# Two feed-forwards with seven-product tiles: products accumulated in one bank, a norm factor carried by the next epsilon

## The reference, cut to what matters

```python
hn = rmsnorm(h, pre_ffn_norm)
ff = (jax.nn.silu(hn @ w_gate) * (hn @ w_up)) @ w_down
h = h + rmsnorm(ff, post_ffn_norm)
e = rmsnorm(p @ w_ple_proj, ple_norm)
gate = jax.nn.sigmoid(h @ w_ple_gate + b_ple_gate)
h = h + e * gate
```

## Time and profile before

| | us |
|---|---|
| median of 3 runs | 1558.11 |
| the runs | 1557.65 to 1559.58 |
| span of the profiled execution | 1558.7 |
| PE busy in it | 1535.3 |
| DVE busy | 1064.5 |
| ACT busy | 715.5 |
| first feed-forward, seven-product tiles | 554.5 to 705.7 |
| second feed-forward, first matmul of its units | about 1144 |

### The profile page before, as it was taken

One profiled execution on the slowest core, in us unless ns is written; L12 is line 12 of the kernel. 1 busy time (PEld: TensorE's weight loads), 2 busy tenths in 40 slices (PEclk: granted clock), 3 DMA queues, 4 the chain that ended last, 5 costly groups with the idle time before them and its releaser, 6 DMA issues.

```text
span 1558.7 us, 19501 instructions
## 1 busy us (share of the span) xinstructions
PE 1535.3 (98%) x7464; PEld 1270.6 (82%) x7464; DVE 1064.5 (68%) x1657; ACT 715.5 (46%) x1069; POOL 133.7 (9%) x131
## 2 busy tenths in 40 slices
PE   8999899999999999999999999999999999999998
PEld 3788677877888899998888787878888888888877
DVE  8998898898888799995753456766476444432356
ACT  5543578764543656653333325446354322222233
POOL 0111000000000111110021011100201101000000
PEclk9999999999999999999999999999999999999999
DMA  9778222233666546657333323111332222323331
GB/s 367 183 187 206 69 94 61 75 95 93 210 238 203 163 127 158 157 148 253 98 110 101 108 85 109 55 41 41 115 132 99 95 95 95 108 86 101 98 135 68
DMA packets 59709, 197.18 MB, mean 127 GB/s; under 512 B 7005, under 2 KB 9309, under 8 KB 59234
## 3 DMA queue, kind: packets, MB, share of 16 engines
q1 hardware_dynamic: 52208, 175.49, 34.3%
q0 software_dynamic: 7408, 20.46, 6.6%
q10 hardware_dynamic: 2, 0.00, 0.0%
HBM read 171.80 MB, written 6.30 MB: 114 GB/s over the span
## 4 chain that ended last, share of the span: by engine, by line
PE 89%; DVE 7%; ACT 2%; issue 1%; DMA 1%; ACTq 0%; POOL 0%; DVEq 0%; POOLq 0%
PE bank L1822 22%; PE bank L1814 22%; PE bank L1815 22%; PE bank L1852 3%; PE bank L1844 3%; PE bank L1843 3%; DVE convout L2430 2%; PE bank L1870 2%; DVE tmp L2501 1%; PE bank L1882 1%; PE bank L1884 1%; PE bank L1883 1%; PE bank L1957 1%; PE bank L1974 1%; DVE spl L2376 1%
## 5 line engine op out<-in xcount | busy, mean ns | idle before, releaser
L1814 PE MATMUL bank<-HH,sph 128*128 128x512 f32 x1192 | 475.7, 399 | 6.9 <-DVE spl L2376 4.7
L1815 PE MATMUL bank<-HH,spl 128*128 128x512 f32 x1192 | 466.0, 391 | 0.0
L2376 DVE TENSOR_TENSOR spl<-raw,sph 128x1024 fp32r<-128x1024 f32 (+1 forms) x206 | 259.8, 1263 | 225.0 <-ACT sph L2032 224.9
L2032 ACT ACTIVATE sph<-raw 128x1024 fp32r<-128x1024 f32 (+1 forms) x227 | 233.0, 1029 | 176.6 <-PE bank L1822 139.5
L1822 PE MATMUL bank<-HL,sph 128*128 128x512 f32 x1192 | 309.7, 394 | 0.0
L1814 PEld LDWEIGHTS bank<-HH,sph 128*128 128x128 f32 x1192 | 225.0, 189 | 58.9 <-issue 10.2
L1815 PEld LDWEIGHTS bank<-HH,spl 128*128 128x128 f32 x1192 | 224.9, 189 | 47.8 <-issue 1.5
L1822 PEld LDWEIGHTS bank<-HL,sph 128*128 128x128 f32 x1192 | 222.7, 188 | 48.6 <-issue 2.4
L2430 DVE SCALAR_TENSOR_TENSOR convout<-convin,vecs,convout 128x512 f32<-128x512 f32 x240 | 165.3, 748 | 0.0
L1814 PE MATMUL bank<-midh,sph 128*128 128x512 f32 x352 | 136.9, 389 | 0.0
L1815 PE MATMUL bank<-midh,spl 128*128 128x512 f32 x352 | 136.9, 389 | 0.0
(11 more groups left out here) (362 smaller groups left out, 2281.0 us busy)
## 6 DMA issues: line engine op xcount, KB each, us to landing
raw<-in_w_in SPq DMA_DIRECT2D x69, 512.0 KB, 3.6
raw<-in_w_up SPq DMA_DIRECT2D x66, 512.0 KB, 3.5
more<-in_w_ada SPq DMA_DIRECT2D x32, 512.0 KB, 5.0
raw<-in_w_down SPq DMA_DIRECT2D x32, 512.0 KB, 3.5
raw<-in_w_gate SPq DMA_DIRECT2D x22, 512.0 KB, 3.2
spl<-raw POOLq DMA_DIRECT2D x18, 512.0 KB, 6.0
ada<-in_w_ada SPq DMA_DIRECT2D x16, 512.0 KB, 10.9
raw<-in_w_down SPq DMA_DIRECT2D x16, 384.0 KB, 3.1
```

The costliest lines, as they stand in the source:

```text
L1814: e.matmul(P_[b][:], sph(n)[:, q], hi[:, k, :], start=k == 0, stop=False)
L1815: e.matmul(P_[b][:], spl(n)[:, q], hi[:, k, :], start=False, stop=False)
L2032: e.activation(sph(n), raw(n), ACT.Copy).then_inc(*up("s_w_high", ("wh", n)))
L2376: e.tensor_tensor(spl(n), raw(n), sph(n).bitcast(F32), ALU.subtract).then_inc(*up("s_w_low", ("wl", n)))
```

## The change

- The second feed-forward gets seven-product tiles too, tiles 4 to 17 (`SEVEN`).
- The seven products of a tile come in the order 0, 3, 2, 4, 5, 1, 6 (`SEVEN_STEP`). Products 0, 2, 5 and 6 are accumulated in one half bank, 3 and 4 in another, 1 beside it. Between them the running sum is copied out (`seven_first`, `seven_third_copy`, `seven_second` on ACT) or added (`seven_up` on DVE), and the next product of that sum waits for it. Two pairs of banks take turns. `factors` makes the factors in the new order; the gate unit's raw buffer is given back later.
- In the second feed-forward `seven_full` makes the scaled x for the T sums, eight instructions on ACT, four behind the root and four behind unit 4; `halves_2(n)` hands out the T sums behind units 3 to 6 and `seven_third` behind 5 and 7. The T operands lie on x, so x is written to DRAM before (`x_spill_all`, SP) and read back after (`x_reload(2)`, POOL).
- Up is no longer multiplied by r (`up_`). The down product is then ff / r, and the same result comes from the epsilon EPS / r^2 in its norm, which `eps_row` stores; `rsqrt` takes it for the name `ff`. In the seven-product tiles `seven_row` multiplies the gate by r.
- The embedding's squares go from the up stage to the down stage, read from a copy that is loaded again from DRAM (`e_copy`, SP).

```diff
-SEVEN = {1: (3, 18)}
+SEVEN = {1: (3, 18), 2: (4, 18)}
+SEVEN_STEP = (0, 3, 2, 4, 5, 1, 6)
 SEVEN_SUMS = (2, 3, 4)
-SEVEN_BANK = ((0, 0), (1, 0), (1, 1), (2, 1), (3, 1), (2, 0), (3, 0))
...
     def factor_low(st, s):
         add("seven_low", st["which"], s)
-        if s % 7 == 6:
+        if s % 7 >= 5:
             load()
+
+    def factor_high(st, s):
+        add("seven_high", st["which"], s)
+
+    def factor_sum(st, s):
+        add("seven_sum", st["which"], s)
 
     def factors(st, count):
         while st["made"] < min(count, st["total"]):
             s = st["made"]
-            if s % 7 in SEVEN_SUMS:
-                add("seven_sum", st["which"], s)
-                if s % 7 == 4:
-                    load()
-            add("seven_high", st["which"], s)
-            if s % 7 == 4:
+            pos = s % 7
+            if pos == 2:
+                factor_sum(st, s)
+                factor_sum(st, s - 1)
+                factor_high(st, s - 1)
+            elif pos == 3:
+                factor_sum(st, s)
+            if pos != 1:
+                factor_high(st, s)
+            if pos in (3, 4):
                 factor_low(st, s - 2)
-            if s and s % 7 != 3:
+            if s and pos not in (2, 3):
                 factor_low(st, s - 1)
...
-    def rsqrt(name, src, n, scale, after):
-        v, q, r = scratch(n), scratch(n), scratch(n)
-        add("rsqrt", name, src, v, q, r, n, scale, after)
+    def rsqrt(name, src, n, scale, after, eps=None):
+        v = scratch(3 * n)
+        q, r = v + n, v + 2 * n
+        add("rsqrt", name, src, v, q, r, n, scale, after, eps)
...
+        r = rsqrt(ss.name, ss.sums(b), T, 1.0 / width, [("cols", ss.name)], eps_row if ss.name == "ff" else None)
...
+        def sum_bank(i):
+            return banks[i % 2]
+
+        def pair_bank(i):
+            return banks[2 + i % 2]
+
+        def settle(pos, i):
+            if pos == 0:
+                add("seven_gate", which, i, pair_bank(i)[0], gate[i])
+            elif pos == 1:
+                add("seven_row", which, i, gate[i])
+            elif pos == 2:
+                add("seven_silu", which, i, gate[i])
+            elif pos == 3:
+                add("seven_mid", which, i, f0 + i, sum_bank(i)[0], gate[i], up[i])
+                tmp.give(up[i], ("seven_mid", which, i))
+            elif pos == 4:
+                add("seven_mid_high", which, i, f0 + i, gate[i])
+            elif pos == 5:
+                add("seven_mid_low", which, i, f0 + i, gate[i])
+                tmp.give(gate[i], ("hi", f"m{which}", f0 + i), ("lo", f"m{which}", f0 + i))
...
         for s in range(total):
-            i, step = divmod(s, 7)
+            i, pos = divmod(s, 7)
+            if pos == 1:
+                gate[i], free = tmp.take()
+                add("seven_first", which, i, sum_bank(i)[0], gate[i], free)
+            elif pos == 2:
+                up[i], free = tmp.take()
+                add("seven_third_copy", which, i, pair_bank(i)[0], up[i], free)
+            elif pos == 3:
+                add("seven_second", which, i, sum_bank(i)[0], gate[i])
+            elif pos == 5:
+                add("seven_up", which, i, sum_bank(i)[0], up[i])
+            if i:
+                settle(pos, i - 1)
             factors(st, s + 6)
             W["cut"] = max(W["cut"], st["first"] + (st["made"] + 1) // 2)
...
-            if step == 5 and i + 2 < f1 - f0:
+            if pos == 5 and i + 2 < f1 - f0:
                 add("seven_third", which, i + 2)
...
+            add("seven", which, s, sum_bank(i), pair_bank(i))
...
-        if which == 2:
-            jobs = [(*job[:3], e_squares) if 4 <= n < 13 else job for n, job in enumerate(jobs)]
-        if not st:
-            gemms(jobs, acts, 1 + which, hook=hook)
-            return
         f0, f1 = SEVEN[which]
...
+        def halves_2(n):
+            if n in (2 * f0 - 3, 2 * f0 - 1):
+                add("seven_third", which, (n - 2 * f0 + 3) // 2)
+            if n == 3:
+                add("seven_t_sum", which, 0)
+                add("seven_t_sum", which, 1)
+                add("seven_t_high", which, 0)
+            elif n == 4:
+                add("seven_t_low", which, 0)
+                add("seven_t_sum", which, 3)
+                add("seven_t_high", which, 1)
+            elif n == 5:
+                add("seven_t_low", which, 1)
+                add("seven_t_sum", which, 2)
+                add("seven_t_high", which, 3)
+            elif n == 6:
+                add("seven_t_low", which, 3)
+                add("seven_t_high", which, 2)
+                add("seven_t_low", which, 2)
...
+        if which == 1:
+            gemms([(*job[:3], lambda n=n: halves(n)) for n, job in enumerate(jobs[:2 * f0])], acts, 2,
+                  table="silu_table")
+        else:
+            gemms([(*job[:3], lambda n=n: halves_2(n)) for n, job in enumerate(jobs[:2 * f0])], acts, 3, hook=hook)
...
     def ffn_rows():
         ss = SumSq("x4")
         for i in range(8):
             ss.add(("XT", i), [("x", 4, i)])
+        add("x_spill_all")
         yield 2
         r = root_of(ss, D)
+        add("eps_row", eps_row, r - 8)
+        for i in range(4):
+            add("seven_full", 2, i)
 
...
         rate[0] = 0
+        for i in range(4, 8):
+            add("seven_full", 2, i)
...
         for i in range(8):
-            sse.add(("EE", i), [("e", i)])
+            sse.add(("EC", i), [("e_copy",)])
...
-    e_sums = e_sum()
-
-    def e_squares():
-        next(e_sums, None)
...
+    add("x_reload", 2)
     ssf = SumSq("ff")
     for i in range(8):
+        if i == 1:
+            add("e_copy")
+            side.append(e_sum())
+            rate[0] = 1
         if i == 7:
+            flush()
+            rate[0] = 0
             add("root_table", keepc(1))
         gemm("w_down", i, NFT, "m2", branch("FFO", i, ssf))
...
+            def x_spill_all():
+                w.wait_ge(at("x_back", 1), *[at("x", 4, i) for i in range(8)])
+                e.dma_start(A["x_scratch"], XT[:]).then_inc(
+                    *up("d_xs2", *[("x_spilt", 2, i) for i in range(8)], by=16))
+
+            def e_copy():
+                w.wait_ge(at("e_spilt"), at("e0_spilt"), *fenced("d2"))
+                e.dma_start(EC[:], A["e_scratch"]).then_inc(*up("d_ec", ("e_copy",), by=16))
...
+            def seven(which, s, sums, pairs):
+                i, step = s // 7, step_of(s)
+                whole_sum, pair = P_[sums[0]][:, 0:256], P_[pairs[0]]
+                to = {1: pair[:, 0:256], 3: pair[:, 256:512], 4: pair[:, 256:512]}.get(step, whole_sum)
+                begins = step in (0, 1, 3)
+                if step == 0:
+                    w.wait_ge(*(each(sums[1]) if i < 2 else [at("seven_mid", which, i - 2)]))
+                elif step == 3:
+                    w.wait_ge(*(each(pairs[1]) if i < 2 else [at("seven_gate", which, i - 2)]))
+                elif step == 2:
+                    w.wait_ge(at("seven_first", which, i))
+                elif step == 4:
+                    w.wait_ge(at("seven_third_copy", which, i))
+                elif step == 5:
+                    w.wait_ge(at("seven_second", which, i))
+                elif step == 6:
+                    w.wait_ge(at("seven_up", which, i))
...
             def seven_full(which, i):
+                if which == 2:
+                    w.wait_ge(at("x", 4, i), *fenced("f2"))
+                    e.activation(PF[:, i, :], XT[:, i, :], ACT.Copy, scale=vec("g_pf", i)).then_inc(
+                        *up("s_cut_a", ("full", 2, i)))
+                    return
...
+                if which == 2:
+                    w.wait_ge(at("e_spilt"))
...
+
+            def eps_row(a, v):
+                w.wait_ge(at("rs1", "x4"))
+                e.tensor_scalar(keep(a, T), sm(v, T), EPS, None, ALU.mult).then_inc(*up("s_scale", ("eps_row",)))
 
...
             def seven_t_sum(which, t):
-                w.wait_ge(*[at("full", i) for i in range(8)], *[at("lo", "n2", i) for i in range(8)], at("e0_spilt"),
-                          *[at("x_spilt", i) for i in range(8)])
+                w.wait_ge(*[at("full", which, i) for i in range(8)], *[at("x_spilt", which, i) for i in range(8)])
+                if which == 1:
+                    w.wait_ge(*[at("lo", "n2", i) for i in range(8)], at("e0_spilt"))
+                else:
...
+                if step == 2:
                     w.wait_ge(at("raw", n + 1), at("seven_third", which, s // 7))
                     ins = e.tensor_tensor(to, raw_half(n + 1, 0), raw_half(n + 1, 1), ALU.add)
-                elif s % 7 == 3:
+                elif step == 3:
+                    w.wait_ge(at("raw", n), at("seven_sum", which, s + 1))
+                    ins = e.tensor_tensor(to, sum_of(which, s + 1), raw_half(n, 0), ALU.subtract)
+                else:
                     w.wait_ge(at("raw", n), at("seven_sum", which, s - 1))
```

(32 more changed lines are left out.)

198 lines of the change are left out of this document (77 added, 121 removed).

## The result

The changed kernel takes 1566.95 us (median of 4 runs, 1566.47 to 1567.23) against 1558.62 for the kernel before: ratio 1.0051, 95% interval 1.0037 to 1.0064. The prediction was 1555.5 with 1561.5 as its upper end. The change costs 8.3 us where a gain of 2.6 was forecast. The profiled execution took 1566.47, with a span of 1564.7 us.

The account below looks back on a forecast made before the run. TensorE, busy 1535.3 of 1558.7 us, was taken as the bound. 1558.7 - 11.2 + 0.6 + 7.2 + 0.8 = 1556.1 us for the profiled execution, 1555.5 for the median; range 1548.0 to 1561.5.

Parts of the forecast that it names:

- Term 1: Products of the second feed-forward's 14 tiles: 10.08 instead of 10.88 us a tile, 11.2 us less.
- The rule of the smaller gap: The skill page's isolated matmul gap, N/2.4 + 2.5 ns, applied to the 14 tiles: 16.6 us saved in all.
- R2: Rival: all step-in cost is hidden, or tiles take 9.6 us; 1546.9 to 1549 us, chance 0.12.
- Term 2: Steady seven-product tiles: the new order's waits for running-sum copies all fit; no cost, 10.08 us a tile kept.
- R3: Rival: in steady tiles a later adding DMA holds PE each tile; 1564.2 us at 0.3 a tile, chance 0.08.
- Term 3: Stepping into the first feed-forward's tiles: third product waits for the copy of product one; 0.6 us.
- Term 4: Stepping into the second feed-forward's tiles: PE waits at unit 7, second and third product, plus adding DMAs; 7.2 us.
- R1: Rival: the second feed-forward's step-in costs half or less, 4 us; 1551.5 us, chance 0.32.
- drain: Skill page's 1.38 us at every ScalarE table switch; not expected here, if real the step-in sum 1.4 us higher.
- Moved and hidden: Spill and reload of x, weight loads, root, embedding's squares and transposes: zero each; 2 us if the copy's cover were gone.
- R4: Rival: the spill of x lands at 1183.9, 6 us after the first T sum wants it; 1561.5 us, chance 0.06.
- Term 5: Low clock behind the second feed-forward's step-in waits: 0.8 us taken, bounds 0 and 2.1.

Follow-up runs that it names:

- e9: e7 with POOL holding the low parts of the second and third undivided unit until VectorE's T sum is done; 1553.01 us.
- e3: Changed kernel with the second feed-forward's first four full products queued ahead of the norm row's root instead of behind it; 1563.10 us.
- e1: Changed kernel with the second feed-forward given back its old schedule, so the new one is in the first only; 1564.94 us.
- e2: Changed kernel with the older tile's banks handed out first where a stage's seven-product tiles end; 1560.87 us.
- e8: e1 with the edit of e2 added (new schedule in the first feed-forward only, exit's banks reordered); 1560.57 us.
- e4: Changed kernel with the embedding's sums (transposes into columns and root) four pieces later in the second feed-forward's down stage; 1564.86 us.
- e11: e7 with the last undivided tile's multiply and rounding queued behind the first seven-product tile's second product; 1556.07 us.
- e7: Changed kernel with the edits of e2, e3, e4 and e6, and both step-in adding transfers one weight unit earlier; 1553.31 us.
- e5: The changed kernel itself, unaltered, measured again; 1566.01 us.
- e6: Changed kernel with the third and fourth T low parts of the second feed-forward moved behind the first tile's weight sums; 1561.78 us.

## Why the prediction was wrong

**Term 1, products: right.** 11.1 to 11.4 by the balance above, 10.9 by e9 (U7 to Y 149.05 instead of 158.25, with 1.72 of waits in it), against 11.2. The rule of the smaller gap that I weighed beside it (16.6 in all) is refuted for this kernel, and R2 with it. (R2 had a slip besides: the 1550.1 that this rule gives lies outside R2's own 1546.9 to 1549.)

**Term 2, steady state: right.** R3, the adding transfer, is refuted: PE is gapless in both stretches. Only the very first tile waited for it (0.88; I had given 0.3 with a bound of 1.9). DVE's row of the sum that held `seven_up` there:

```profile
1209.96 0.69 DVE L2746 TENSOR_TENSOR sums<-raw 128x512 f32<-128x512 f32 x1 [2.88 <-DMA raw<-raw]
```

**Term 3, first step-in: right.** 0.64 against 0.6.

**Term 4, second step-in: right in kind, and right in sum by luck.** Unit 7: 1.61 against 2.0. Second product: 3.65 against 2.8 + 0.3. Third: 0.40 against 1.8. Adding transfer 0.88 against 0.3. Together 6.54 against 7.2. Up to the first T sum the forecast held to 0.2 us, once the 4.74 us by which U3 now comes later are taken off: the full products began at 1171.83 - 4.74 = 1167.09, the first Silu at 1179.09 - 4.74 = 1174.35 (forecast 1174.5), the first T sum at 1182.77 - 4.74 = 1178.03 (1177.9). Two steps behind it failed. I took both engines' durations as they are alone: three T operations at 1.23, of which two took 2.21 and 2.32 (1184.03 and 1192.32 in the changed kernel), some 2 us of DVE queue. The trace of before shows it, and I had not read those rows. DVE's rows there with POOL at work and with POOL idle, and POOL's:

```profile
1183.08 1.37 DVE L2382 TENSOR_TENSOR tmp<-tmp,tmp 128x512 f32<-128x512 f32 x1 [1.22 <-ACT tmp L2047]
...
1187.41 0.69 DVE L2382 TENSOR_TENSOR tmp<-tmp,tmp 128x512 f32<-128x512 f32 x1 [1.22 <-ACT tmp L2047]
...
1182.61 1.30 POOL L3061 TENSOR_TENSOR midl<-tmp,midh 128x512 fp32r<-128x512 f32 x1 [4.02 <-ACT midh L2243]
```

The Trainium skill (GPSIMD Engine Reference, Key points) says that GpSimd shares its SBUF interfaces with VectorE, with contention for instructions that have two SBUF inputs. The rows agree: both T sums and this square-sum have two such inputs.

And I followed the queues of DVE and ACT but not the banks: unit 5 needs the bank of unit 0's gate, whose reader the full products hold up (e3). That gave 1.40, in no term. R1 asked for a step-in of at most half and falls. The table load brought no drain here either: it starts at 1177.80, where the full product ahead of it ends (1175.23 + 2.55).

**"Moved and hidden", the step that cost most.** Zero for each, and the list did not have the exits at all. The exit of the first feed-forward's tiles costs 2.95 and mostly 1.7 of clock behind it (e1, e2, e8). The rule that I left out: a diff that changes which bank holds what also changes the order in which banks go back to the ring. `SEVEN_BANK`, struck out in the diff, was the place to ask. Second, "its four transposes cost the same there": they made PE wait 0.80 (e4). The rest of that paragraph was right. The spill of x landed 13.2 us after its issue at 1164.48, at 1177.7, and the first T sum began at 1182.77 with 0.20 of idle time ahead of it; R4 is refuted. Squares, copy, reloads: no wait.

**Term 5, the clock: too small.** 0.8 for one wait. There were two stretches more than before, 3.4 us. Two of the three lie behind waits (2.95 and 3.65); the third, at 1512, lies behind none, and what brings it on stays open.

**The sum.** -11.2 + 0.6 + 7.2 + 0.8 = -2.6 was forecast; found: -11.2 + 12.3 + 3.4 = +4.5 of +5.3 from M to the end. With the wait of 0.55 that is gone, 1.3 is left over. What the waits cost beyond their brackets may be that: at 0.2 to 0.3 each, an estimate from the two read above, eight waits give 1.6 to 2.4. Missing waits (2.95 + 1.40 + 0.80) make 5.15 of the difference, the clock 2.6. The base was also off a little: run times lie 2.1 us over the spans for the kernel before, 1.8 for the changed one, and the profiled execution of before (1558.7) was 2.0 above the median span of later ones (1556.7 of 23). That is why the medians differ by 8.3 and the profiles by 6.0. In which stretch the kernel before was 2.0 slow is not known, as no other execution of it has a trace; so the landmarks explain the 6.0, and some 2 us of the 8.3 are placed nowhere.

**The rivals.** Neither of the two that ended slower was it. Both looked for a resource that runs late in every tile, or a transfer; what happened were one-off waits at three borders, each short.

## What to carry to other kernels

When a stage gets a new inner loop, price its two borders as carefully as its steady state: write down for each side who holds every bank, buffer and queue slot at the border and which one is handed out next; a first-in-first-out ring must be refilled in the order in which its members really come free. Waits of different places added up here and could be mended one by one, but a wait taken away by delaying work is only gone if what stands behind the delayed work is also named (e11). Where medians differ by 1 to 2 us, compare the list of waits and the time from a landmark behind the shared part as well, and remember that a trace is one execution, which can lie 3 us off its kernel's median (e4).

## What the runs showed of the hardware

VectorE and GpSimd hold each other up when they run at once and the VectorE instruction has both inputs in SBUF: a T sum of 128x1024 takes 1.23 us alone and 2.21 to 2.32 beside a GpSimd subtraction, which itself takes 1.85 instead of 1.29; moving the subtraction by 2 us restores 1.23 and 1.22 (e9) and slows the neighbour that it meets next from 1.21 to 1.94. The rows fit one engine standing still until the other is done, rather than both running slower: in e7 the subtraction from 1175.26 ends at 1177.11, the T sum beside it at 1178.19, 1.08 later; the next from 1183.98 ends at 1185.50, its T sum at 1186.58, again 1.08 later, where a T sum alone takes 1.23. No run tests this reading. A multiply with one input in PSUM kept its 0.68 beside GpSimd (e9).

The clock behind a wait is not a fixed price. The same wait of 2.95 to 2.96 us was followed by 0.54 and 0.60 of the full clock in the changed kernel, with low clock behind it in e1, e3, e5 and e6 too, and by 1.00 in e4, which is the same up to there. A wait of 1.42 at 1025 in the kernel before was followed by 0.83 and 0.74 over two windows of 4 us, and the same wait in the changed kernel by 1.00. A stretch of it costs 1.7 us in every kernel here; twice two came in a row (e4, e11). There were also low-clock stretches with next to no idle time ahead, such as the one from 1512 to 1516 of the changed kernel, behind a window with PE busy 3.94 of 4.00:

```profile
1508.00:1512.00 4.00, 3.94 (x26) 3.21 (x25) 1.09 (x3) 1.75 (x3) 1.02 (x1) 1.00 0.55 160
1512.00:1516.00 4.00, 4.00 (x10) 1.87 (x9) 3.48 (x6) 1.26 (x2) 1.33 (x1) 0.57 0.86 336
```

What brings that one on stays open.
